# Second attention of a two-block transformer kernel: softmax bookkeeping of two heads in one VectorE instruction each

## The reference, cut to what matters

```python
def mla_attention(c_q, c_kv, k_pe, positions, ...):
    ...                                  # q, k (B,S,8,192) normalized, v (B,S,8,128)
    scale = QK_DIM ** -0.5
    for s0 in range(0, S, Q_BLOCK):      # 8 blocks of 128 queries
        e = s0 + Q_BLOCK
        s = jnp.einsum("bqhd,bkhd->bhqk", q[:, s0:e], k[:, :e]).astype(jnp.float32) * scale
        mask = jnp.arange(e)[None, :] <= (s0 + jnp.arange(Q_BLOCK))[:, None]
        p = jax.nn.softmax(jnp.where(mask, s, -jnp.inf), axis=-1).astype(v.dtype)
        outs.append(jnp.einsum("bhqk,bkhd->bqhd", p, v[:, :e]))
    o = jnp.concatenate(outs, axis=1).reshape(B, S, N_HEADS * V_DIM)
    return o @ w_mla_o
```

## Time and profile before

| | |
|---|---|
| median of 3 runs | 3402.25 us |
| the three runs | 3403.94, 3400.33, 3402.25 us |
| span of the profiled execution | 3399.7 us, first to last instruction |
| VectorE busy | 1291.8 us, 38% |
| TensorE busy | 2890.0 us, 85% |
| ScalarE busy | 869.3 us, 26% |
| the attention stage, scores to last weighing | about 2300 to 2563 us |

### The profile page before, as it was taken

How to read it: one execution, slowest core, us unless ns; L and a number is a source line. 1 busy time by engine, 2 the same in 40 slices (tenths; PEclk the granted TensorE clock), 3 DMA queues, 4 the chain that set the end, 5 groups by cost and what they waited for, 6 DMA issues and landing times. The chain is left out here.

```text
span 3399.7 us, 42056 instructions
## 1 busy us (share of the span) xinstructions
PE 2890.0 (85%) x16732; PEld 1832.9 (54%) x16732; DVE 1291.8 (38%) x2499; ACT 869.3 (26%) x1446; POOL 313.1 (9%) x490
## 2 busy tenths in 40 slices
PE   5999989778969999985899989787898886887782
PEld 2888667556833333335777868344567773332231
DVE  5321088665731111117365121455554452111112
ACT  5211055573100000005355111333334210100001
POOL 0210000001000111002000000220001101111112
PEclk8999999988979999997999999898999988989996
DMA  7222197043379999976311312200004529999995
GB/s 273 55 81 81 56 414 308 28 147 106 114 299 382 405 405 392 405 292 252 88 44 38 106 65 81 72 8 1 1 1 155 178 108 408 420 421 420 418 415 231
DMA packets 200691, 694.43 MB, mean 204 GB/s; under 512 B 28835, under 2 KB 76886, under 8 KB 150086
## 3 DMA queue, kind: packets, MB, share of 16 engines
q1 hardware_dynamic: 160470, 587.46, 44.5%
q0 software_dynamic: 27520, 75.53, 5.8%
q10 hardware_dynamic: 12528, 29.01, 2.2%
HBM read 579.02 MB, written 138.07 MB: 211 GB/s over the span
## 5 line engine op out<-in xcount | busy, mean ns | idle before, releaser
L2414 PE MATMUL exp_ps_g<-exp_raw,exp_xT 128*32 128x512 f32 x3072 | 337.4, 597 | 9.5 <-ACT exp_xT L2460 9.5
L2659 PE MATMUL exp_ps_g<-exp_gu,exp_xT 128*64 128x512 f32 x1024 | 264.5, 676 | 91.1 <-DMA exp_gu<-in_exp_w 85.9
L2414 PEld LDWEIGHTS exp_ps_g<-exp_raw,exp_xT 128*32 128x32 f32 x3072 | 116.8, 110 | 214.1 <-issue 199.6
L2659 PEld LDWEIGHTS exp_ps_g<-exp_gu,exp_xT 128*64 128x64 f32 x1024 | 87.9, 154 | 247.3 <-issue 215.7
L724 PE MATMUL inproj_ps<-inproj_w_low,h1T_high 128*128 128x512 f32 (+1 forms) x448 | 178.8, 399 | 9.7 <-DVE inproj_w_low L434 9.7
L726 PE MATMUL inproj_ps<-inproj_w_high,h1T_high 128*128 128x512 f32 (+1 forms) x448 | 175.4, 392 | 0.0
L725 PE MATMUL inproj_ps<-inproj_w_high,h1T_low 128*128 128x512 f32 (+1 forms) x448 | 174.5, 390 | 0.0
L2438 PE MATMUL exp_ps_y<-exp_raw,exp_hT 128*32 128x512 f32 x1536 | 169.8, 592 | 0.8 <-DVE exp_hT L2504 0.8
L2497 DVE TENSOR_TENSOR exp_h<-exp_sg,exp_ps_g 128x512 f32<-128x512 f32 x24 | 26.0, 1085 | 342.2 <-ACT exp_sg L2466 342.2
L2757 DVE TENSOR_TENSOR exp_h<-exp_sg,exp_ps_g 128x256 f32<-128x256 f32 x32 | 19.6, 611 | 342.3 <-ACT exp_sg L2713 342.3
L2438 PEld LDWEIGHTS exp_ps_y<-exp_raw,exp_hT 128*32 128x32 f32 x1536 | 59.4, 110 | 105.7 <-issue 104.7
(11 more groups left out here) (541 smaller groups left out, 5817.2 us busy)
## 6 DMA issues: line engine op xcount, KB each, us to landing
exp_gu<-in_exp_w SPq DMA_DIRECT2D x64, 2048.0 KB, 29.6
exp_raw<-in_expert_w_gate SPq DMA_DIRECT2D x64, 1024.0 KB, 16.3
exp_raw<-in_expert_w_up SPq DMA_DIRECT2D x64, 1024.0 KB, 16.8
exp_raw<-in_expert_w_down SPq DMA_DIRECT2D x64, 1024.0 KB, 14.5
exp_dn<-in_exp_w SPq DMA_DIRECT2D x32, 2048.0 KB, 27.1
scratch_y<-da_zero SPq DMA_DIRECT2D x1, 32768.0 KB, 149.4
scratch_y<-da_zero SPq DMA_DIRECT2D x1, 24576.0 KB, 68.0
open_slab<-in_w_ada SPq DMA_DIRECT2D x16, 1024.0 KB, 14.5
```

The costliest lines, as they stand in the source:

```text
L2414: last = nc.tensor.matmul(ps_g[lane, z], xT[:, n % 2, k, lane], raw[:, of_lane[l], j * F:(j + 1) * F], start=(k == 0), stop=(k == KD - 1))
L2659: last = nc.tensor.matmul(ps_g[side(e)], xT[:, m.par, k, side(e)], gu[:, m.buf, :, e, k, :], start=(k == 0), stop=(k == KD - 1))
```

## The change

In `maximum`, mask, maximum and bias are made for both units of a pair with one instruction each, after a wait for the scores of both; one instruction then signals both biases. In `divide`, the reciprocal is made for both units at once, after a wait for both exponentials, while the scaling stays one instruction per unit. In the order of VectorE's work both scalings now stand before the second `copy_turned` of the pair, where the second one stood behind it.

```diff
                 def divide(n):
                     m = n % HELD
-                    dve.wait_ge(e_done, n + 1)
-                    ch.link(V.reciprocal(ls[:, m, 1:2], ls[:, m, 0:1]))
+                    dve.wait_ge(e_done, n + 2)
+                    ch.link(V.reciprocal(ls[:, m:m + 2, 1], ls[:, m:m + 2, 0]))
                     keys = slice(0, (units[n][0] + 1) * P)
-                    V.tensor_scalar(p[:, m, keys], p[:, m, keys], ls[:, m, 1:2], None, ALU.mult).then_inc(scaled, 1)
+                    for x in (m, m + 1):
+                        V.tensor_scalar(p[:, x, keys], p[:, x, keys], ls[:, x, 1:2], None, ALU.mult).then_inc(scaled, 1)
 
                 def maximum(n):
                     qt, h = units[n]
                     b = n % HELD
-                    dve.wait_ge(s_done, n + 1)
-                    diag = ps[:, n % 2, qt * P:(qt + 1) * P]
-                    ch.link(V.tensor_tensor(diag, diag, bar[:], ALU.add))
-                    ch.link(V.reduce_max(st[:, b, 0:1], ps[:, n % 2, 0:(qt + 1) * P], AX_X))
-                    V.scalar_tensor_tensor(st[:, b, 1:2], st[:, b, 0:1], -1.0, rq[:, qt, h:h + 1], ALU.mult, ALU.mult).then_inc(nb_ready, 1)
+                    dve.wait_ge(s_done, n + 2)
+                    diag = ps[:, :, qt * P:(qt + 1) * P]
+                    ch.link(V.tensor_tensor(diag, diag, bar[:].unsqueeze(1).broadcast_to([P, 2, P]), ALU.add))
+                    ch.link(V.reduce_max(st[:, b:b + 2, 0], ps[:, :, 0:(qt + 1) * P], AX_X))
+                    V.scalar_tensor_tensor(st[:, b:b + 2, 1], st[:, b:b + 2, 0], -1.0, rq[:, qt, h:h + 2], ALU.mult, ALU.mult) \
+                        .then_inc(nb_ready, 2)
 
                 for n in range(0, len(units) + LAG + 2, 2):
                     if n > LAG:
                         read_results(n - LAG - 1)
-                    for m in range(2):
-                        if LAG <= n < len(units) + LAG:
-                            copy_turned(dve, V.tensor_copy, 1, n - LAG + m)
-                        if 2 <= n < len(units) + 2:
-                            divide(n - 2 + m)
+                    if LAG <= n < len(units) + LAG:
+                        copy_turned(dve, V.tensor_copy, 1, n - LAG)
+                    if 2 <= n < len(units) + 2:
+                        divide(n - 2)
+                    if LAG <= n < len(units) + LAG:
+                        copy_turned(dve, V.tensor_copy, 1, n - LAG + 1)
                     if n < len(units):
-                        for m in range(2):
-                            maximum(n + m)
+                        maximum(n)
```

## The result

The changed kernel took 3425.93 us (median of 4 runs, 3421.96 to 3429.29), the kernel before 3401.29 us (median of 4). The ratio is 1.0067, with an interval from 1.0055 to 1.0079: slower by 0.67%, where I had forecast 0.42% and a range that ended at 3424. The profiled execution's span is 22.2 us longer than that of the earlier trace rows.

A forecast was written before the change was run, and what follows sets the result against it. TensorE's waits for ScalarE's exponentials and copy, which hang on the bias, were taken as the bound. Delays of `weigh`, 3.60 us over eight tiles, times four pairs, 14.4 us, on 3402.25 gave 3416.7 us; range 3406 to 3424.

The forecast's parts named there:

- First exponential: ScalarE's first exponential of a pair: later by 0.26 us at tile 0 and 1.20 us at tile 7.
- Second exponential: ScalarE's second exponential, queued behind the first: later by 0 us at tile 0 up to 0.75 us at tile 7.
- What `weigh` sees: Start of `weigh` on TensorE: the later route decides, 0.14 to 0.97 us a pair, 14.4 us in all.
- plain route: From first mask to `weigh`: first exponential, `plain_scores`, `weigh` behind it; later by R - 0.03 us (R: one unit's reduction) less slack.
- copy route: From first mask to `weigh`: second exponential, ScalarE's copy, `weigh`; ends last before the edit, later by 0 to 0.75 us.
- my fourth rival: Before `weigh`: only the copy route counts, 12 us, 3414.2 us; counted with the forecast, no chance of its own.
- The wait for both scores: Before a pair's mask: the two score signals come together, taken as nothing; 0.1 us a pair, 3 us, kept in range.
- Reciprocal and order of work: VectorE's paired reciprocal and both scalings before the second copy: costed at nothing, covered by TensorE's own matmuls.
- The clock: TensorE's granted clock: nothing in the sum; prediction wrong if tiles 0 to 2 differ by more than a pair or two.
- The faster one: Loop goes by the second bias alone: each pair wins 0.46 us, 14.7 us in all, 3387.5 us; chance 0.06.
- That the edit doesn't do what it says: VectorE's pair instruction no cheaper than two: about 10 us on top of the sum, 3427 us; chance 0.02.
- More clock lost: TensorE in early tiles: 1.2 GHz lasts through five more pairs, 6.5 us more, 3423 us; chance 0.10.

The follow-up runs named there:

- copy_early: Kernel before, with ScalarE's copy of the first unit's transposes moved between a pair's two exponentials; 3384.50 us, ratio 0.9936.
- joint_wait: Kernel before, with the first mask of a pair waiting for the scores of both units; 3406.56 us, ratio 1.0010.
- div_only: Kernel before, with only the reciprocals paired and both scalings put before the second copy; 3402.75 us, ratio 0.9996.
- mask_only: Kernel before, with only the mask paired after a wait for both units; 3396.68 us, ratio 0.9982.

## Why the forecast was right in direction and too small

*What bounds the kernel: right.* TensorE's wait for ScalarE, which hangs on the bias, set each pair; VectorE's busy time was worth nothing.

*Prices: right.* The pair's mask took 0.43 us (0.42 to 0.43 forecast), the pair's maximum over 2048 columns 2.29 (2.29), the bias 0.16.

*First exponential: right, 0.07 us small.* +3.06 instead of +2.99 in tile 7. The bias starts 0.10 us after the end of a reduction with two results, where it started 0.03 us after one with a single result.

*Second exponential: right, some 0.05 us small.* It starts straight behind the first and is later by 0.80 us in tile 7 where I had 0.75.

*What `weigh` sees: the sum near, its split wrong, so luck.* I had the plain route decide in tiles 0 to 2 and 5 to 7, with slacks of 0.12 us in tile 0, 0.46 in tile 4 and 0.23 in tile 7. `copy_early` measured 0.45, 0.66 and 0.42: `weigh` gets going sooner behind `plain_scores` than I had read, because its first weights are loaded under it. The copy route decides up to tile 6, and both in tile 7, nearly as my fourth rival had it. By that route alone I had 12.0 us, and up to tile 6 nearly every pair came out 0.09 to 0.10 us above it (0.05 in the second exponential, 0.04 in the wait for both scores). The error in the plain route (too dear) and what was missing in the other nearly cancel: 14.4 forecast, 15.1 measured. The forecast had named as a sign of being wrong that `weigh` follows something else than `plain_scores` at tiles 5 to 7; in tiles 5 and 6 it does.

*The wait for both scores: taken as nothing, 0.04 us a pair,* 1.3 us in all, measured alone in `joint_wait` and contained in the 15.1. It was inside the 3 us I kept for it.

*Reciprocal and order of work: right.* Nothing, measured alone in `div_only`.

*The clock: the step that failed.* I put the change of clock at nothing, gave more half-clock time a chance of 0.10, and looked for it in tiles 0 to 2. I argued that tile 1 already had 1.00 with TensorE busy for 4.13 of 5.30 us and that later tiles are denser. Density over a pair was the wrong thing to look at: the second pair of tile 7 is denser, busy for 10.95 of 12.80 us at a clock of 1.00 in the first trace, and in two other traces of the same code the clock fell in it. What the edit changes is the longest idle time, the one ahead of `plain_scores`: 1.42 to 1.96 us in tiles 2 to 7, where it was 0.31 to 1.11. In four traces of the changed kernel the time from first to last mask was longer than before by 16.2, 16.0, 21.0 and 19.5 us; less the 14.2 of longer pairs, the clock took 2.0, 1.8, 6.8 and 5.3 us, 4.0 on average. Of this 3.2 to 4.6 us fell in tiles 2 to 7; the rest, from -1.5 to +2.2 us, lies in tiles 0 and 1, where the kernel before is at half clock too, and may be chance. Behind the last mask the clock took another 1.9 us on average. The price I gave such time, 1.3 us a pair, compared two different pairs of tile 1; the same pair with and without a fall differs by 1.3 to 1.7 us. The Trainium skill, TensorE: Matmul & The Clock Gate, section Why this matters for your kernels, names idle gaps between bursts of matmuls as what lets the clock fall. I had given that too little weight; the traces agree with it in kind, though the page warns of longer gaps than the 1.64 to 1.96 us before the falls here.

*What stays open.* The means of all executions differ by 21.6 us (17 of the changed kernel, 3424.7 us; 71 of the kernel before, 3403.1 us). Of these 14.2 are the 31 distances, 0.8 the last pair, 4.0 the clock between the masks and 1.9 the clock behind the last one, 20.9 in all. The 24.6 us between the first four executions of each are 3 us more, and the remaining 0.7 us are less than the scatter: single executions of the changed kernel range from 3411.5 to 3434.8 us, and the time of the first mask alone varies by up to 10 us in identical code. It is not known why the clock falls in pair 7.0 of one execution and in 7.1 or not at all in another, although the idle time is the same. No run settled in the medians what the clock is worth, so its share rests on the traces alone.

*Rivals.* The faster one (the second bias alone counts) is out for this edit: `mask_only` shows that the bias counts as long as the first exponential is hardly delayed, 0.16 us a pair. That the edit doesn't do what it says is out too, by the row of 2.29 us. More clock lost was the right rival, in the wrong tiles.

## What to carry to other kernels

A pair of items in a pipeline of engines gives its first result after one item and its second after two; an instruction over both gives neither before the second. Weigh the fixed cost that goes (some 0.16 us an instruction here) against the time for which the first consumer now waits (one whole reduction, up to 1.2 us), and join only what is short beside its fixed cost and ahead of both: the mask alone, 128 columns, gained 0.16 us a pair.

Before shortening the engine that seems to be waited for, follow the loop round to the last thing that ends. Here it was a copy queued behind the second exponential without need. Moving it took 0.64% off the kernel without any change to VectorE (0.9936, 0.9922 to 0.9949), about as much as the edit lost, and that version beats both kernels.

An added wait can be dearer than its length if it makes TensorE's longest idle time longer, here from at most 1.11 to up to 1.96 us in tiles 2 to 7. Compare the granted clock pair by pair, not over the stage.

## What the hardware did that I had not expected

- The vector reduction with two results lets its follower start 0.10 us after its end; the one with a single result, 0.03 us (both behind a wait on the same semaphore). It is so at every length, from 256 to 2048 columns and from 128 to 1024.
- TensorE loads the first weights of a later group of matmuls under the last matmul of the one before: 1.40 us after the start of `plain_scores`, where the matmuls took 1.98.
- The same code took from 2300.7 to 2311.0 us up to the first mask, while the pairs of the attention repeat to 0.02 us wherever the clock is the same. Inside one trace a change of 0.04 us a pair is plain to see; in the time of the whole program one of 3 us is not.
